# Second expert layer: where the dots' gelu stands in ScalarE's program, and how thinly token steps are laid beside the choices

## The chip, the core and the metric

The kernel runs on one core of a Trainium2 chip, as one program for the whole model. The metric is the device time of one execution in microseconds (us); the number compared is the median of several executions.

## What is computed

The program runs a small transformer over 256 tokens of width 1024. Its last stage is a "peer" layer: every token chooses 128 of 16384 experts (8 heads, 16 each), and each expert is one row of a table `u` and one row of a table `v`.

```python
def peer(h, w_q, sub_keys, u, v):
    T, D = h.shape
    q = (h @ w_q).reshape(T, PEER_HEADS, 2, PEER_QDIM // 2)
    s = jnp.einsum('thpd,hpnd->thpn', q, sub_keys)
    sv, si = lax.top_k(s, PEER_TOPK)
    cand = (sv[:, :, 0, :, None] + sv[:, :, 1, None, :]).reshape(T, PEER_HEADS, PEER_TOPK * PEER_TOPK)
    fv, fi = lax.top_k(cand, PEER_TOPK)
    ...
    idx = (i1 * PEER_NKEYS + i2).reshape(T, PEER_HEADS * PEER_TOPK)
    g = jax.nn.softmax(fv, axis=-1).reshape(T, PEER_HEADS * PEER_TOPK)
    def chunk(args):
        hc, ic, gc = args
        ue = u[ic]
        ve = v[ic]
        act = jax.nn.gelu(jnp.einsum('td,ted->te', hc, ue), approximate=False)
        return jnp.einsum('te,ted->td', gc * act, ve)
```

After it, `x = x + g2 * f` and a last RMS norm give the output.

## The kernel before

The change is in `split_experts`, the last stage (it is called by `peer_1`). It computes the layer in two ways at once.

**Dense half (tokens 128 to 255).** TensorE multiplies the tokens by the whole of `u`: 128 *up tiles* of 128 x 1024 float32 (512 KB each, `rise(e)`, line 2823), ScalarE applies gelu to each product (line 2914), and then TensorE multiplies by the whole of `v`: 128 *down tiles* of 512 KB (`fall(r)`, line 2840). Up and down tiles come through a ring of four slots, in order, by SyncE's queue (`fetch`); tile j may be fetched once tile j-4 has been used. Between the two, the activations are multiplied by gates. Gates are made four tokens at a time, in 64 steps n: VectorE writes 0/1 marks (`mark(n)`, lines 2727 to 2735), TensorE multiplies them (`gates(n)`, line 2836), VectorE multiplies the activations by the result (`weigh(n)`, line 2743). Steps 0 to 31 (the first 64 experts' keys) belong to the rise, and TensorE's program has them spread behind up tiles 74 to 125: `gates(n)` stands behind up tile 74 + 53n/32. Steps 32 to 63 stand behind down tiles 0 to 54. `mark(n)` waits for `gates(n-2)`, `weigh(n)` for `gates(n)`.

**Gathered half (tokens 0 to 127).** For each of a token's 128 choices, GpSimd's queue gathers one row per token: 128 rows of 4 KB, 512 KB in one indirect DMA (line 2594). In the first table (`u`) VectorE multiplies the gathered rows by the tokens and sums: a *dot* (line 2608). In the second table (`v`) it adds the rows, weighted, to an accumulator: an *accumulation* (line 2616 for the first, 2619 for the others). Both are called *token steps*; there are 128 of each, strictly in order. The gathers go round five buffers (`ROWS` = 5): gather n is issued when step n-5 is done, whatever table it belongs to. Between the two, ScalarE applies gelu to the 128 dots (line 2924), and VectorE multiplies by the softmax weights (line 2612).

**The choices.** Before the marks VectorE finds the top 16 of every row of scores (`sixteen`, `level`, `choices`), for 2 x 4 groups. The first four groups make the indices that the gathers need. Beside this work a counter, `spend`, lays in token steps: every instruction adds its columns + 150 to `spent`, and when that reaches 1200 a dot is issued.

What holds others up in the order of the programs: ScalarE waits ahead of gelu 64 (`AT_SCORES`) until the last `level` is done, because the activations from there on overwrite the scores. Ahead of gelu 70 (`EXP_AT`) it waits for the end of the choices. TensorE waits behind up tile 72 (`SELECTED`) for the softmax weights, VectorE ahead of the marks for the turned choices. TensorE may be at most two up tiles ahead of ScalarE's gelus. The down tiles wait for all 128 gelus and the first 32 gate steps. VectorE lays token steps between the gate steps: 1 + (n % 3 < 2) in each of n = 0 to 31, dots only; 1 + n % 2 from n = 32; the rest stand in a loop behind n = 64. Then come the sums of the dense half, `turned_back` (TensorE turns the accumulator, line 2879), the sum of squares (`sum_squares`, line 426) and the norm.

Of the kernel before, what the change touches and what calls it, by code (L numbers as in the profile page):

```python
# [21 lines left out]
ACT = mybir.ActivationFunctionType  # L22
# [3 lines left out]
P = 128  # L26
# [18 lines left out]
ROWS = 5  # L45
# [404 lines left out]
def rstd_ends(k):  # L450

    for name in ("mean_square", "inverse_mean", "rstd"):
        k.count(name).ends(1)
# [2063 lines left out]
def split_experts(k, a, layer, S, finish):  # L2517

    nc, HP, NT, B, R = k.nc, 2 * HEADS, T // P, 4, RING
    DENSE, G = T - S, HEADS // 2  # L2520
    N, Q, STEPS, HALF = NKEYS, 2 * HEADS, DENSE // 4, NKEYS // 2
    U, V = Q, Q + NKEYS
    wq, u, v = a.peer_q[layer], a.peer_u[layer], a.peer_v[layer]
    rows_of = (a.peer_rows, a.peer_v.rearrange("l a b d -> (l a b) d"))
# [15 lines left out]
    idx, act_of, coef = k.rows[0:S, 1, 0:P].bitcast(U32), k.rows[0:S, 1, P:2 * P], k.rows[0:S, 1, 2 * P:3 * P]  # L2540
    first_row = k.rows[0:S, 1, 3 * P:4 * P]
    whole_ctx = k.ctx[:].rearrange("p c t -> p (c t)")
    bufs = [b[0:S] for b in (whole_ctx[:, 0:D], whole_ctx[:, D:2 * D], k.rows[:, 0], spare[:, 1],
                             k.acts[:].rearrange("p r t -> p (r t)"))]
    marks = k.scratch[:, 0:1280].bitcast(BF16).rearrange("p (r n) -> p r n", r=2)
    second = marks[:, :, 0:512].rearrange("p r (a n t) -> p r a n t", a=2, t=2)
    in_half = marks[:, :, 512:1280].rearrange("p r (m a n t) -> p r m a n t", m=3, a=2, t=2)
# [3 lines left out]
    sums = k.ps[:, 0:4].rearrange("p b (c t) -> p (b c) t", t=T)  # L2551
    back = k.ps[:, 4:8].rearrange("p b (c t) -> p (b c) t", t=T)
    order = [(table, p) for table in range(2) for p in range(P)]
    EXP_AT, SELECTED, FIRST_GATES = 70, 72, 74
    gates_after = [[n for n in range(STEPS) if FIRST_GATES + n * (N - 1 - FIRST_GATES) // STEPS == e] for e in range(N)]
    gates_under = [[n for n in range(STEPS, 2 * STEPS) if (n - STEPS) * (HALF - 8) // STEPS == r] for r in range(N)]
    FINAL, SETTLED, LEVELS, count, picks_made = 0, 0, 0, 0, 0
# [6 lines left out]
    tokens_turned, tokens_kept, ready, used, token_gelu, token_weights, turned_back = map(k.count, (  # L2564
        "tokens_turned", "tokens_kept", "choices_ready", "row_used", "token_gelu", "token_weights", "turned_back"))
# [7 lines left out]
    with nc.Block() as block:  # L2573
        @block.sync
        def _(sp):
            for j in range(R, Q):
                k.fetch(sp, j, 0, wq[j])
            for e in range(N):
                k.fetch(sp, U + e, 0, u[e])
            for e in range(N):  # L2580
                k.fetch(sp, V + e, 0, v[:, e])
            for n in range(KD // 2):
                c = slice(2 * n, 2 * n + 2)
                sp.wait_ge(normed.sem, normed.after(2 * n + 2))
                sp.dma_start(k.out[:, c], k.x[:, c]).then_inc(stored.sem, 16)
            sp.wait_ge(stored.sem, stored.after(16 * (KD // 2)))

        @block.gpsimd
        def _(pool):
            for n, (table, p) in enumerate(order):  # L2590
                if not table and p % 32 == 0:
                    pool.wait_ge(ready.sem, ready.after(p // 32 + 1))
                pool.wait_ge(used.sem, used.after(n + 1 - ROWS))
                nc.gpsimd.indirect_dma_start(bufs[n % ROWS], None, rows_of[table],
                                             bass.IndirectOffsetOnAxis(idx[:, p:p + 1], 0)).then_inc(k.row_loaded[n % ROWS].sem, 16)

        @block.vector
        def _(dve):
            step, spent, units = 0, 0, 0

            def token_step():

                nonlocal step
                n, b = step, step % ROWS
                table, p = order[n]
                dve.wait_ge(k.row_loaded[b].sem, k.row_loaded[b].after(16 * (n // ROWS + 1)))
                if not table:
                    nc.vector.tensor_tensor_reduce(bufs[b], bufs[b], tok, 1.0, 0.0, ALU.mult, ALU.add,  # L2608
                                                   act_of[:, p:p + 1]).then_inc(used.sem, 1)
                elif p == 0:  # L2610
                    dve.wait_ge(token_gelu.sem, token_gelu.after(1))
                    nc.vector.tensor_tensor(coef, coef, weight[0:S, 0:HEADS].rearrange("p n b -> p (n b)"),
                                            ALU.mult).then_inc(token_weights.sem, 1)
                    dve.wait_ge(token_weights.sem, token_weights.after(1))
                    dve.wait_ge(used.sem, used.after(n))
                    nc.vector.tensor_scalar(tok, bufs[b], coef[:, p:p + 1], None, ALU.mult).then_inc(used.sem, 1)
                else:
                    dve.wait_ge(used.sem, used.after(n))
                    nc.vector.scalar_tensor_tensor(tok, bufs[b], coef[:, p:p + 1], tok, ALU.mult, ALU.add).then_inc(used.sem, 1)  # L2619
                step += 1  # L2620

            def spend(columns):

                nonlocal spent
                if units:
                    spent += columns + 150
                    if spent >= 1200 and step < min(P, 32 * units):
                        spent -= 1200
                        token_step()

            def sixteen(rows, src, rest, values, places, arrive):
# [106 lines left out]
            def weigh(n):  # L2738

                h, n_of_half = n // STEPS, n % STEPS  # L2740
                acts = A[:, h * HALF:(h + 1) * HALF, n_of_half * B:(n_of_half + 1) * B]
                dve.wait_ge(product.sem, product.after(n + 1))
                nc.vector.tensor_tensor(acts, acts, k.ps[:, gate_bank(n), 0:B * HALF].rearrange("p (t n) -> p n t", t=B),
                                        ALU.mult).then_inc(kept.sem, 1)
# [29 lines left out]
            for n in range(2 * STEPS + 1):  # L2774
                if n < 2 * STEPS:
                    mark(n)
                if n:
                    weigh(n - 1)
                for _ in range(1 + (n % 3 < 2) if n < STEPS else 1 + n % 2):
                    if step < (P if n < STEPS else len(order)):  # L2780
                        token_step()
            while step < len(order):
                token_step()
            for c in range(KD):
# [101 lines left out]
        @block.scalar  # L2886
        def _(act):
            def take(j):

                act.wait_ge(done.sem, done.after(j + 1))  # L2890
                nc.scalar.activation(q[:, j], k.ps[:, j % R, 0:T], ACT.Copy).then_inc(taken.sem, 1)

            def move(p):

                act.wait_ge(scored.sem, scored.after(p + 1))
                nc.scalar.activation(s.rearrange("p (t r) n -> p t r n", t=NT)[:, :, 2 * p:2 * p + 2].rearrange(
                    "p t r n -> p t (r n)"), k.ps[:, 6 + p % 2].rearrange("p (t n) -> p t n", t=NT), ACT.Copy).then_inc(moved.sem, 1)

            take(0)
            act.wait_ge(tokens_turned.sem, tokens_turned.after(1))  # L2900
            for n in range(2):
                nc.scalar.activation(tok[:, n * 4 * P:(n + 1) * 4 * P], k.ps[0:S, 4 + n], ACT.Copy).then_inc(tokens_kept.sem, 1)
            for j in range(1, Q):
                take(j)
                if j >= 3 and j % 2:
                    move(j // 2 - 1)
            for e in range(N):
                if e == AT_SCORES:
                    act.wait_ge(top.sem, top.after(LEVELS))
                if e == EXP_AT:  # L2910
                    act.wait_ge(after.sem, after.after(SETTLED))
                    nc.scalar.activation(weight, weight, ACT.Exp).then_inc(exps.sem, 1)
                act.wait_ge(done.sem, done.after(U + e + 1))
                nc.scalar.activation(A[:, e], k.ps[:, 4 + e % 2, 0:DENSE], ACT.Gelu).then_inc(acted.sem, 1)  # L2914
                if e == 0:
                    move(HEADS - 1)
                if e == SELECTED:
                    for w in range(3):
                        act.wait_ge(transposed.sem, transposed.after(3 * NT))
                        nc.scalar.activation(k.picks[:, :, w],  # L2920
                                             k.ps[:, 6 + w // 2, w % 2 * T:w % 2 * T + T].rearrange("p (s t) -> p s t", t=B),
                                             ACT.Copy).then_inc(picked.sem, 1)
            act.wait_ge(used.sem, used.after(P))
            nc.scalar.activation(coef, act_of, ACT.Gelu).then_inc(token_gelu.sem, 1)
            for c in range(KD):
                act.wait_ge(settled.sem, settled.after(c + 1))
                square_x(k, c, 1)
            root_of_inverse(k, act)
# [19 lines left out]
    for c in (turned_back, settled, normed, k.count("squares")):  # L2948
        c.ends(KD)
    rstd_ends(k)  # L2950
    for b in range(ROWS):
        k.row_loaded[b].ends(16 * len(range(b, len(order), ROWS)))
    tables.ends(16)
    stored.ends(16 * (KD // 2))
    k.ring_ends(V + N, 0)
# [254 lines left out]
```

## Time and profile before

| | us |
|---|---|
| median of 3 runs | 3766.13 (3762.77 to 3767.57) |
| the profiled execution | 3757.47 |
| its span, first to last instruction | 3755.7 |
| `split_experts`, from about 2984 to the end of the span | 772 |
| TensorE busy over the span | 3287.2 (88%) |
| VectorE busy | 2497.0 (66%) |
| ScalarE busy | 874.4 (23%) |
| DMA | 983.68 MB, mean 262 GB/s |

The times in rows are microseconds from the start of the span. The span is a single profiled execution, 8.66 us faster than the median of the timed ones, and 1.8 us of it lie outside the span. The busy share of an engine over the whole span says little of the last stage, so the stage is read in windows.

### The profile page before, as it was taken

To read this page: it belongs to the slowest core of one execution; us is meant where nothing else is said; L and a number is where in the kernel's file an instruction comes from. 1 tells how busy PE (TensorE), PEld (TensorE's weight loads), DVE (VectorE), ACT (ScalarE), POOL (GpSimd) and SP (SyncE) were. 2 spreads that over 40 slices of the span, in tenths; PEclk is the share of its full clock that TensorE was granted. 3 is DMA by queue.
4 is the path that set the end of the run, shared out by engine and by line. 5 is a ranking of instruction groups with operands and counts; after the bars stand their busy time and mean duration, and the time that the engine had idled before them with its cause. 6 is when DMAs were issued, how large, how long until landed. Compare 5 with 4: busy or idle time off the path is not lost. (4 is left out here: it accounts for less than half of the span.)

```text
span 3755.7 us, 56484 instructions
## 1 busy us (share of the span) xinstructions
PE 3287.2 (88%) x22342; PEld 2862.1 (76%) x22359; DVE 2497.0 (66%) x4759; ACT 874.4 (23%) x1601; POOL 883.1 (24%) x804
## 2 busy tenths in 40 slices
PE   9998999998999978999499987778879897599876
PEld 9976999986997657887388866666657687488875
DVE  5556656555664364589988857767775488877745
ACT  4345434334443353111022200000014411110000
POOL 0000000000000001014555545555530033423432
PEclk9999999999999999999799999999999999899998
DMA  7652666642662204279899999999971289999998
GB/s 245 224 176 101 234 222 205 230 160 90 230 211 84 73 1 152 73 234 394 306 355 369 363 364 403 400 403 404 404 290 49 97 336 409 349 361 342 406 409 316
DMA packets 298406, 983.68 MB, mean 262 GB/s; under 512 B 32928, under 2 KB 66720, under 8 KB 297248
## 3 DMA queue, kind: packets, MB, share of 16 engines
q1 hardware_dynamic: 187552, 577.36, 43.6%
q0 software_dynamic: 110592, 402.70, 27.6%
q8 instruction: 179, 2.93, 0.3%
q14 instruction: 83, 0.68, 0.1%
HBM read 960.01 MB, written 19.92 MB: 261 GB/s over the span
## 5 line engine op out<-in xcount | busy, mean ns | idle before, releaser
L325 PE MATMUL banks<-h_whole,ring 128*128 128x256 f32 (+1 forms) x4352 | 782.6, 336 | 138.0 <-ACT acts_out L2459 54.0
L325 PEld LDWEIGHTS banks<-h_whole,ring 128*128 128x128 f32 x4352 | 677.1, 193 | 214.4 <-ACT big L2914 84.7
L300 DVE TENSOR_TENSOR ring_lo<-ring,ring_hi 128x1024 fp32r<-128x1024 f32 x365 | 448.0, 1228 | 370.4 <-ACT ring_hi L294 351.1
L325 PE MATMUL banks<-scratch,ring 128*128 128x256 f32 x2048 | 490.1, 396 | 126.6 <-DVE scratch L2269 126.3
L325 PEld LDWEIGHTS banks<-scratch,ring 128*128 128x128 f32 x2048 | 392.8, 196 | 224.0 <-DVE scratch L2269 171.2
L294 ACT ACTIVATE ring_hi<-ring 128x1024 fp32r<-128x1024 f32 x365 | 386.7, 1059 | 571.1 <-PE banks L315 512.2
L325 PE MATMUL banks<-big,ring 128*128 128x128 f32 x2048 | 260.8, 281 | 50.7 <-DMA ring<-peer_v_dram 47.8
L311 PE MATMUL banks<-h_parts,ring_hi 128*128 128x256 f32 x1160 | 287.2, 286 | 6.0 <-PEq L664 3.4
L325 PEld LDWEIGHTS banks<-big,ring 128*128 128x128 f32 x2048 | 238.0, 192 | 70.2 <-DMA ring<-peer_v_dram 66.8
L312 PE MATMUL banks<-h_parts,ring_hi 128*128 128x256 f32 x1160 | 283.8, 282 | 0.0
L311 PEld LDWEIGHTS banks<-h_parts,ring_hi 128*128 128x128 f32 x1160 | 221.7, 191 | 18.3 <-issue 17.8
L984 POOL TENSOR_TENSOR scratch<-ctx_t 128x256 f32<-128x256 f32 x8 | 7.9, 991 | 929.7 <-POOLq L609 929.7
L312 PEld LDWEIGHTS banks<-h_parts,ring_hi 128*128 128x128 f32 x1160 | 221.7, 191 | 0.3
L2104 POOL DMA_INDIRECT x_t<-peer_rows_dram,rows x103 | 129.5, 1258 | 346.0 <-DVE rows L2218 211.6
L311 PE MATMUL banks<-h_parts_ctx,ring_hi 128*128 128x256 f32 x768 | 189.9, 285 | 4.3 <-ACT ring_hi L294 4.3
L312 PE MATMUL banks<-h_parts_ctx,ring_hi 128*128 128x256 f32 x768 | 187.7, 282 | 0.0
L2134 DVE SCALAR_TENSOR_TENSOR h_whole<-x_t,rows,h_whole 128x1024 f32<-128x1024 f32 x102 | 130.8, 1284 | 57.4 <-DMA x_t<-peer_v_dram,rows 57.0
L2134 DVE SCALAR_TENSOR_TENSOR h_whole<-ctx_t,rows,h_whole 128x1024 f32<-128x1024 f32 x101 | 129.8, 1285 | 57.2 <-DMA ctx_t<-peer_v_dram,rows 56.7
L315 PE MATMUL banks<-h_parts,ring_lo 128*128 128x256 f32 x1160 | 163.0, 283 | 0.1
L312 PE MATMUL banks<-hidden_parts,ring_hi 128*128 128x256 f32 x672 | 162.9, 281 | 0.0
L311 PE MATMUL banks<-hidden_parts,ring_hi 128*128 128x256 f32 x672 | 162.8, 281 | 0.0
L311 PEld LDWEIGHTS banks<-h_parts_ctx,ring_hi 128*128 128x128 f32 x768 | 146.6, 191 | 13.8 <-issue 13.5
(366 smaller groups left out, 5852.5 us busy)
## 6 DMA issues: line engine op xcount, KB each, us to landing
ring<-peer_u_dram SPq DMA_DIRECT2D x256, 512.0 KB
ring<-peer_v_dram SPq DMA_DIRECT2D x256, 512.0 KB
big<-mod_w_dram SPq DMA_DIRECT2D x96, 512.0 KB, 4.6
ring<-ffn_gate_dram SPq DMA_DIRECT2D x88, 512.0 KB
ring<-ffn_up_dram SPq DMA_DIRECT2D x88, 512.0 KB
ring<-ffn_down_dram SPq DMA_DIRECT2D x88, 512.0 KB
ring<-peer_q_dram SPq DMA_DIRECT2D x32, 512.0 KB
act_store<-acts_out SPq DMA_DIRECT2D x128, 128.0 KB
```

The lines of the kernel that those rows point to most:

```text
L294: self.nc.scalar.activation(self.hi[:, n % 2], self.ring[:, self.slot(j)], ACT.Copy).then_inc(self.count("tile_hi").sem, 1)
L300: self.nc.vector.tensor_tensor(self.lo[:, self.slot(j)], self.ring[:, self.slot(j)], self.hi[:, n % 2].bitcast(F32), ALU.subtract).then_in ...
L311: self.nc.tensor.matmul(out, w, b_hi, start=opens and m == 0, stop=False)
L312: self.nc.tensor.matmul(out, w, b_lo, start=False, stop=False)
L315: ins = self.nc.tensor.matmul(out, self.lo[:, self.slot(j), c * P:(c + 1) * P], b_hi, start=False, stop=opens and m == last)
L325: ins = self.nc.tensor.matmul(out, self.ring[:, self.slot(j), c * P:(c + 1) * P], b, start=opens and m == 0, stop=opens and m == len(terms ...
L984: k.nc.gpsimd.tensor_tensor(to, norm.src[:, c], norm.src[:, c], ALU.mult).then_inc(squared.sem, 1)
L2104: nc.gpsimd.indirect_dma_start(bufs[n % ROWS], None, rows_of[n // TOKEN_STEPS], bass.IndirectOffsetOnAxis(idx[:, t, p:p + 1], 0)).then_inc ...
L2134: nc.vector.scalar_tensor_tensor(tok[:, t], bufs[b], coef[:, t, p:p + 1], tok[:, t], ALU.mult, ALU.add).then_inc(used.sem, 1)
```

## The change

Four edits, all in `split_experts`. The number of gather buffers is taken from the list `bufs` (which has five) and not from `ROWS` (which is 5). `spend` issues a dot each 1500 and not each 1200. In the marks' loop, each n has 1 + (n % 3 < 2) token steps throughout; at n = 20 all dots that are left are done; accumulations may begin at n = 24. ScalarE's gelu of the dots stands behind gelu 112 of the up tiles and not behind the last.

```diff
@@ -2542,6 +2542,7 @@
+    W = len(bufs)
@@ -2551,7 +2552,7 @@
-    EXP_AT, SELECTED, FIRST_GATES = 70, 72, 74
+    EXP_AT, SELECTED, FIRST_GATES, GELU_AT, DOTS_BY = 70, 72, 74, 112, 20
@@ -2590,9 +2591,9 @@
             for n, (table, p) in enumerate(order):
                 if not table and p % 32 == 0:
                     pool.wait_ge(ready.sem, ready.after(p // 32 + 1))
-                pool.wait_ge(used.sem, used.after(n + 1 - ROWS))
-                nc.gpsimd.indirect_dma_start(bufs[n % ROWS], None, rows_of[table],
-                                             bass.IndirectOffsetOnAxis(idx[:, p:p + 1], 0)).then_inc(k.row_loaded[n % ROWS].sem, 16)
+                pool.wait_ge(used.sem, used.after(n + 1 - W))
+                nc.gpsimd.indirect_dma_start(bufs[n % W], None, rows_of[table],
+                                             bass.IndirectOffsetOnAxis(idx[:, p:p + 1], 0)).then_inc(k.row_loaded[n % W].sem, 16)
@@ -2624,8 +2625,8 @@
                 if units:
                     spent += columns + 150
-                    if spent >= 1200 and step < min(P, 32 * units):
-                        spent -= 1200
+                    if spent >= 1500 and step < min(P, 32 * units):
+                        spent -= 1500
                         token_step()
@@ -2776,9 +2777,11 @@
                     mark(n)
                 if n:
                     weigh(n - 1)
-                for _ in range(1 + (n % 3 < 2) if n < STEPS else 1 + n % 2):
-                    if step < (P if n < STEPS else len(order)):
+                for _ in range(1 + (n % 3 < 2)):
+                    if step < (P if n < DOTS_BY + 4 else len(order)):
                         token_step()
+                while n == DOTS_BY and step < P:
+                    token_step()
             while step < len(order):
                 token_step()
@@ -2914,14 +2917,15 @@
                 if e == 0:
                     move(HEADS - 1)
+                if e == GELU_AT:
+                    act.wait_ge(used.sem, used.after(P))
+                    nc.scalar.activation(coef, act_of, ACT.Gelu).then_inc(token_gelu.sem, 1)
                 if e == SELECTED:
                     ...
-            act.wait_ge(used.sem, used.after(P))
-            nc.scalar.activation(coef, act_of, ACT.Gelu).then_inc(token_gelu.sem, 1)
```

The other hunks put `W` for `ROWS` in the buffer's number and in the semaphores' last counts.

## Rows read from the trace of the kernel before

**Rows 1.** The page's slices of the span: DMA's busy share in 40 slices.

```profile
DMA  7652666642662204279899999999971289999998
```

**Rows 2.** Windows: stretch, length, busy (count) of each engine, PEclk, DMA share, GB/s.

```profile
3080.00:3200.00 120.00, 93.30 (x738) 85.90 (x739) 102.60 (x293) 12.86 (x47) 45.67 (x47) 1.00 1.03 409
...
3218.00:3250.00 32.00, 3.57 (x24) 3.35 (x24) 30.20 (x91) 0.45 (x2) 13.57 (x14) 0.59 0.86 293
3250.00:3281.00 31.00, 22.43 (x145) 21.59 (x144) 27.61 (x67) 6.03 (x14) 15.43 (x15) 0.82 0.95 356
...
3351.00:3406.00 55.00, 53.36 (x597) 52.96 (x597) 23.86 (x71) 7.61 (x28) 0.00 (x0) 1.00 0.82 254
3406.00:3420.00 14.00, 13.21 (x147) 12.89 (x148) 12.74 (x25) 0.08 (x1) 6.76 (x5) 1.00 0.90 316
3420.00:3440.00 20.00, 16.49 (x166) 15.39 (x167) 15.24 (x30) 0.00 (x0) 9.21 (x8) 1.00 1.01 402
3440.00:3460.00 20.00, 17.93 (x183) 16.94 (x182) 16.04 (x31) 0.00 (x0) 8.99 (x7) 1.00 1.00 371
...
3720.00:3736.00 16.00, 6.38 (x51) 5.60 (x49) 11.50 (x10) 0.00 (x0) 5.83 (x5) 0.89 0.83 301
```

**Rows 3.** The same stretch for two lines alone: the gathers (2594), gelu (2914).

```profile
3080.00:3200.00 120.00, 45.67 (x47) 1.00 1.03 409
...
3080.00:3200.00 120.00, 12.86 (x47) 1.00 1.03 409
```

**Rows 4.** Timeline, ScalarE: start, us, what [idle before <-releaser]: gelu 63; 64 and 65.

```profile
3215.54 0.28 ACT L2914 ACTIVATE big<-banks 128x128 f32<-128x128 f32 x1 [2.28 <-PE banks L325]
3248.18 0.45 ACT L2914 ACTIVATE big<-banks 128x128 f32<-128x128 f32 x2 [32.36 <-DVE big L2650]
```

**Rows 5.** Timeline, VectorE beside the choices: dots 1, 17, 75, 79 and 89.

```profile
3031.75 1.23 DVE L2608 CUSTOM_DVE_ANT_0 ctx_t<-ctx_t,h_whole 128x1024 f32<-128x1024 f32 x1 [2.73 <-DMA ctx_t<-peer_rows_dram,rows]
...
3066.06 1.23 DVE L2608 CUSTOM_DVE_ANT_0 ctx_t<-ctx_t,h_whole 128x1024 f32<-128x1024 f32 x1
...
3217.32 1.22 DVE L2608 CUSTOM_DVE_ANT_0 acts_out<-acts_out,h_whole 128x1024 f32<-128x1024 f32 x1
...
3227.40 1.23 DVE L2608 CUSTOM_DVE_ANT_0 h_whole<-h_whole 128x1024 f32<-128x1024 f32 x1 [0.55 <-DMA h_whole<-peer_rows_dram,rows]
...
3248.80 1.22 DVE L2608 CUSTOM_DVE_ANT_0 h_whole<-h_whole 128x1024 f32<-128x1024 f32 x1
```

**Rows 6.** Timeline, VectorE: the last dot, and the weights behind the dots' gelu.

```profile
3339.53 1.22 DVE L2608 CUSTOM_DVE_ANT_0 rows<-rows,h_whole 128x1024 f32<-128x1024 f32 x1
...
3406.18 0.29 DVE L2612 TENSOR_TENSOR rows<-rows,big 128x128 f32<-128x128 f32 x1 [3.81 <-ACT rows L2924]
```

**Rows 7.** Timeline, GpSimd: the sixth gather of the second table.

```profile
3407.53 0.94 POOL L2594 DMA_INDIRECT h_whole<-peer_v_dram,rows  x1 [65.57 <-DVE h_whole L2616]
```

**Rows 8.** Timeline, TensorE: up tiles (16 matmuls each) behind two waits, gates, tiles with data waiting.

```profile
3248.51 10.32 PE L325 MATMUL banks<-h_whole,ring 128*128 128x128 f32 x64 [27.89 <-ACT big L2914]
...
3268.10 3.63 PE L325 MATMUL banks<-h_whole,ring 128*128 128x128 f32 x16 [3.67 <-ACT big L2914]
...
3356.72 3.82 PE L325 MATMUL banks<-h_whole,ring 128*128 128x128 f32 x32
3360.38 0.52 PE L2836 MATMUL banks<-scratch 128*128 128x64 bf16 x12
```

**Rows 9.** Timeline, VectorE: two accumulations in a row, in the marks' loop.

```profile
3425.66 2.67 DVE L2619 SCALAR_TENSOR_TENSOR h_whole<-ctx_t,rows,h_whole 128x1024 f32<-128x1024 f32 x2
```

**Rows 10.** Timeline, TensorE: the last down tile, the turned accumulator, two sums of squares.

```profile
3725.76 2.05 PE L325 MATMUL banks<-big,ring 128*128 128x128 f32 x16 [0.48 <-DMA ring<-peer_v_dram]
...
3736.70 1.97 PE L2879 MATMUL banks<-con,h_whole 128*128 128x128 f32 x8 [8.83 <-DVE h_whole L2619]
3740.84 6.33 PE L426 MATMUL banks<-big,ones 128*128 128x256 f32 x16 [2.17 <-DVE x_t L2789]
...
2973.66 3.72 PE L1794 MATMUL banks<-big,ones 128*128 128x256 f32 x16 [0.49 <-ACT big L1775]
```

More of the change, by code:

```diff
@@ L2603, in token_step @@
                 nonlocal step
-                n, b = step, step % ROWS
+                n, b = step, step % W
                 table, p = order[n]
-                dve.wait_ge(k.row_loaded[b].sem, k.row_loaded[b].after(16 * (n // ROWS + 1)))
+                dve.wait_ge(k.row_loaded[b].sem, k.row_loaded[b].after(16 * (n // W + 1)))
                 if not table:
@@ L2950, in split_experts @@
     rstd_ends(k)
-    for b in range(ROWS):
-        k.row_loaded[b].ends(16 * len(range(b, len(order), ROWS)))
+    for b in range(W):
+        k.row_loaded[b].ends(16 * len(range(b, len(order), W)))
     tables.ends(16)
```

## The prediction

> **What bounds the kernel now.** I read the slices of the page first, then the last stage in windows, then the timelines of single engines where the windows show a hole. The slices show DMA near its full share from slice 33 on, with two dips [rows 1]. In windows the full rate is 409 GB/s, at a DMA share of 1.03, as from 3080 to 3200 [rows 2]. One tile or one gather is 128 x 1024 float32 = 524,288 bytes, so at full rate each costs 524,288 / 409,000 = 1.28 us. I call that a *unit*. The stage moves 128 up tiles, 128 down tiles and 256 gathers, 512 units. That is 656 us of the 772 the stage lasts, so the DMA engines bound it, and a time is won only where they are idle. In 120 us 47 gathers and 47 gelus of up tiles pass [rows 3]: with both queues backed up the two streams share the engines one to one, a tile and a gather in each 2.56 us.
>
> Where DMA is below 409 GB/s, the shortfall over 409 times the length is lost time [rows 2]:
> - 3218 to 3250, 293 GB/s: 32 x 116/409 = 9.1 us; 3250 to 3281, 356 GB/s: 4.0 us. Together **13.1 us**.
> - 3351 to 3406, 254 GB/s: 20.8 us; 3406 to 3420, 316 GB/s: 3.2 us. Together **24.0 us**.
> - 3420 to 3460, 402 and 371 GB/s: **2.2 us**. 3720 to 3736, 301 GB/s: **4.2 us**.
>
> The sum is 43.5 us. The first hole is ScalarE's wait ahead of gelu 64: gelu 63 starts at 3215.54, gelu 64 at 3248.18, released by VectorE's last `level` after 32.36 us idle [rows 4]. TensorE is 27.89 us without work [rows 8], the ring is full, and only gathers are left. The second hole is the dots' gelu: the last dot starts at 3339.53, the weights behind the gelu at 3406.18 [rows 6], the next gather waits 65.57 us [rows 7]. Up tiles alone use 254 of 409 GB/s, since TensorE bounds them: two tiles start at 3356.72 and the gates behind them at 3360.38 [rows 8], so it needs 1.8 us a tile, and about 0.4 for a gate step of 0.52 that overlaps the next tile, against 1.28 of DMA a tile.
>
> **Part 1: dots at 1500.** Counting `spend` through the program: when the last `level` is done, 88 dots stand before it with 1200 and 70 with 1500. At the end of the choices it is 97 and 77, ahead of the marks 103 and 83. Does thinning bring the choices forward? Before, dots 17 to 75 take 3217.32 - 3066.06 = 151.3 us, 2.61 us each, and dots 79 to 89, with no wait for data in between, 21.4 us, 2.14 us each [rows 5]. A dot holds VectorE for 1.15 us (1.22 less the overlap), so 1200 of `spend` are 0.99 us and 1500 are 1.24. Then a dot with its share of the choices takes 2.39 us, still below the 2.6 that the shared DMA allows. So the gathers keep their pace, VectorE uses the idle time that it has beside them, and dot 70 falls where it did: dots 1 to 17 take 0.25 us more each from 3031.75 [rows 5], so dot 16 stands at about 3066.5, and 54 dots at 2.6 us later dot 70 stands at 3207. **The last level is ready at about 3209**, ahead of gelu 64, which up tiles at 2.56 us bring at 3218.1. The wait of 32 us is gone. What is next late? Dot 77, the end of the choices, at about 3226, against gelu 69 at 3231. The exp then waits for nothing, three dots and the shares end near 3236, and TensorE finishes up tile 72 at 3238.5. The marks begin near 3243, up tile 74 needs them at 3244. Each has 2 to 9 us in hand, and a stall below the 3 tiles in the ring (7 us) costs DMA nothing. I take 1 us lost, for a thinner start. W is 5 as before: nothing.
>
> **Part 2: dots by n = 20.** Before, 14 gate steps finish the dots; now 20 leave 117 done, and 11 are drained in n = 20. Up tile 105, behind which gates(19) stands, ends at 3215.5 + 42 x 2.56 = 3323, so the drain starts at 3324. VectorE could do it in 11 x 1.15 = 12.7 us, but the rows come by DMA. TensorE goes on with tiles 106 to 108 and stops at about 3331 for mark 21, which is queued on VectorE behind the drain; the ring fills with 109 to 112. So some 10.5 gathers and 6.5 tiles have to land, 17 units, 21.8 us: **the drain ends at about 3346**, and mark 21 (1.4 us) at 3347.5. TensorE idles 16 us, DMA doesn't. Then four tiles and three gate steps up to gates(23) would take 8.4 us at 1.8 and 0.4. After 27.89 us idle four tiles took 10.32 us, and after 3.67 us idle one took 3.63, where PEclk is 0.59 and 0.82 [rows 2, 8]: the clock was at its lower level (1.2 GHz). I take 12 us: the first accumulation at 3360. In these 14 us from the drain's end, 11 units, DMA has the five gathers of the second table that may be ahead, less one, and some 3 to 4 tiles: **about 4 us lost**. The gelu at 112 itself waits for nothing: tile 112 follows the drain in TensorE's program. It is 0.3 us of ScalarE.
>
> The Trainium skill speaks against such a pause (TensorE: Matmul & The Clock Gate, "The HAM clock gate"): the clock is gated to half while the array is idle and is given back after busy time. By the page the four tiles cost what I took for them and no more; without any gating the 4 us would be 1. The trace agrees in the two rows named.
>
> **Part 3: accumulations from n = 24.** Steps 24 to 31 bring 14 of them beside tiles 113 to 127. A gate step of VectorE's is 23.86 us / 14 steps = 1.7 us in 3351 to 3406, of five instructions each (71 in all) [rows 2], an accumulation 1.33 (2.67 for two) [rows 9]; 1.7 + 5/3 x 1.33 = 3.9 us a step, against 5/3 gathers and 53/32 tiles, 3.3 units, 4.26 us. DMA is full again. The down tiles start near 3394 (before: 3406.9), with 14 accumulations done where there were none. I take 2 us lost at this passage. From n = 32 the gate step has 1.67 accumulations instead of 1.5 and 1.75 tiles: 4.38 us of DMA to 3.9 of VectorE. The small holes of 2.2 us I leave.
>
> **Part 4: the end.** At n = 64 there were 177 token steps done, now 197: 59 left, beside 72 tiles. Before, the down tiles ended first (3727.8) and TensorE waited 8.83 us for the last accumulation [rows 10]. Now gathers end about 12 tiles before TensorE, which then takes 1.8 us a tile instead of 1.28: 12 x 0.52 = **6 us lost**, plus 0.5 us because a last tile takes 1.8 us after landing and a last accumulation 1.3. In exchange TensorE comes to the sum of squares without the 8.8 us pause. It took 6.33 us there and takes 3.72 for the same 16 matmuls elsewhere [rows 10]: 2.6 us won, if the clock is the cause.
>
> **Sum.** Lost before 43.5; lost after 1 + 4 + 2 + 2.2 + 6 + 0.5 = 15.7, and 1 more for what VectorE's lumpy work does to the pace: 16.7. Gain 43.5 - 16.7 + 2.6 = **29.4 us**: 3757.5 - 29.4 = 3728.1 for an execution like the profiled one, whose span would be 3726.3. Against the median of the runs, 8.7 us higher, 3766.1 - 29.4 = **3736.7**.
>
> **Rivals.**
> - *The second hole only moves.* The drain holds TensorE, and then TensorE holds the stage: gathers of the second table come too late to fill anything, as when the drain ends at 3360 and not 3346 because gathers keep to one in 2.56 us (11 x 2.56 = 28 us) with the ring long full. Then DMA idles for 10 us in the drain and 7 behind it, and the gain is 29.4 - 15: 3751. Against it: with the ring full nothing competes with the gathers, and VectorE's dots are at 1.15 us. For it: 3218 to 3250 ran at 293 GB/s with gathers alone [rows 2], though there VectorE had 1 us of choices between dots. Chance 0.14.
> - *The choices are still late* (the change doesn't do what it says at gelu 64). It takes 2.8 us a dot to pass 3218. Each 0.1 us above that costs 5 us of wait, of which DMA loses 0.3. At 3.0 us, 10 us of wait: 4 us lost, within the forecast's own range; that it comes to the old wait would need 3.2. Then the gain is about 16: 3750. Chance 0.05.
> - *Slower: TensorE stays at the lower clock behind the drain.* A tile at that level takes 3.63 us against 2.56 of shared DMA, so each tile beyond the first four costs 1.07. The gain is used up after 29.4/1.07 = 27 tiles, and if it lasts through the marks of the second half (15 + 56 tiles) it costs 76: 3813. Up to 20 tiles it is 3737 to 3758. Against it: after the two waits of before PEclk is 0.59 and 0.82 and then 1.00 again [rows 2]. Chance 0.04 beyond 27 tiles, 0.04 for 10 to 27.
> - *More is won*: the drain starts with several rows landed, no slow tiles behind it, and the streams end together. Lost after is then 7 and the gain 39: 3727, down to 3721. Chance 0.10.
>
> **How the numbers follow.** Forecast (gain 20 to 37 us, 3729 to 3746) 0.60; the cases above 0.37; unnamed 0.03. The range 3721 to 3757 takes in the forecast, the larger gain and the two rivals that keep half of it. A measurement of this kernel tells 0.2%, 7.5 us, from no change. Below 3758.6 lie the forecast, the larger gain and most of the first two rivals: faster 0.86; same 0.07; slower 0.07.
>
> **What would show it.** Gelu 64 in ScalarE's timeline at about 3218 with no idle over 3 us; the last dot at 3345; TensorE idle 14 to 18 us ahead of tile 109; the weights (line 2612) at about 3360; the first down tile near 3394; the last accumulation about 20 us before the last down tile; DMA at 409 GB/s in all windows but those just named. Wrong if the window 3324 to 3346 is below 380 GB/s (first rival), if gelu 64 starts after 3225 (second), or if PEclk is below 1 past 3375 (third).

## The result, and the profile after

The changed kernel takes 3737.4 us in the median of 6 runs (3734.2 to 3742.2), the kernel before 3760.7 (3754.1 to 3767.6, also 6): a ratio of 0.9938, 95% interval 0.9923 to 0.9952, so 23.3 us or 0.6% less. The profiled execution took 3737.35 us with a span of 3735.5.

The spans differ by 20.2 us, but the last stage doesn't start at the same time in each execution. Its first instruction that is easy to find is ScalarE's first copy of the queries. In ScalarE's timeline (columns: start, duration, engine and line, operation, in brackets the idle time ahead and what ended it) it stands, before and after, at

```profile
2991.87 0.39 ACT L2891 ACTIVATE big<-banks 128x256 f32<-128x256 f32 x1 [7.94 <-PE banks L325]
```

```profile
2995.20 0.39 ACT L2894 ACTIVATE big<-banks 128x256 f32<-128x256 f32 x1 [7.94 <-PE banks L325]
```

From there to the end of the span I count the *stage*: 3755.7 - 2991.87 = 763.8 us before and 3735.5 - 2995.20 = 740.3 after. The stage is 23.5 us shorter, about as the medians are, and the 3.3 us lie ahead of it, in work that the change doesn't touch. The experiments below are compared by the stage too, since it leaves that scatter out; but each stage comes from one profiled execution, and its own scatter is known from a single repeat (740.3 and 739.7 us for the changed kernel). Of what stands later in after than in the forecast, 3.3 us are this later start.

Windows of after (columns: the window, its length, busy us and instructions of PE, PEld, DVE, ACT, POOL, then the granted clock, the DMA share and GB/s):

```profile
3036.00:3216.00 180.00, 145.81 (x1105) 134.66 (x1104) 172.72 (x544) 22.81 (x72) 73.18 (x73) 0.99 1.02 406
3216.00:3236.00 20.00, 15.17 (x122) 13.85 (x120) 14.14 (x32) 2.05 (x8) 7.46 (x8) 1.00 1.03 409
3236.00:3256.00 20.00, 17.16 (x163) 16.36 (x164) 15.00 (x36) 6.04 (x14) 8.14 (x8) 1.00 0.97 371
3256.00:3334.00 78.00, 67.30 (x703) 63.23 (x700) 65.10 (x152) 8.33 (x30) 28.87 (x31) 1.00 1.02 407
3334.00:3380.00 46.00, 26.45 (x273) 25.91 (x269) 32.56 (x65) 3.53 (x13) 19.32 (x17) 0.78 0.90 318
3380.00:3420.00 40.00, 35.46 (x356) 33.25 (x356) 32.53 (x61) 2.50 (x9) 15.79 (x15) 1.00 1.02 403
3420.00:3540.00 120.00, 105.52 (x1076) 98.54 (x1076) 100.62 (x181) 0.00 (x0) 61.66 (x46) 1.00 1.02 406
3540.00:3697.00 157.00, 125.53 (x990) 114.18 (x991) 79.09 (x63) 0.00 (x0) 56.65 (x58) 1.00 1.02 406
3697.00:3720.00 23.00, 23.00 (x207) 22.94 (x206) 0.98 (x4) 0.00 (x0) 0.00 (x0) 1.00 0.72 238
```

Lost time again is the shortfall from 409 GB/s over 409, times the length. The two holes of before, 13.1 and 24.0 us [rows 2], are gone. In their place stand 20 x 38/409 = 1.9 us at 3236 to 3256, and 46 x 91/409 = 10.2 us around the drain. The windows at 403 to 407 GB/s lose 4.3 us together. At the end 14 down tiles run alone, and 3697 to 3720 loses 23 x 171/409 = 9.6 us.

ScalarE's timeline is the answer to [rows 4]. Gelu 64 (the second line) has no wait left but for its tile, and the exp ahead of gelu 70 follows gelu 69 at once:

```profile
3219.61 0.28 ACT L2917 ACTIVATE big<-banks 128x128 f32<-128x128 f32 x1 [2.29 <-PE banks L325]
3222.23 0.28 ACT L2917 ACTIVATE big<-banks 128x128 f32<-128x128 f32 x1 [2.34 <-PE banks L325]
...
3235.89 0.28 ACT L2917 ACTIVATE big<-banks 128x128 f32<-128x128 f32 x1 [2.26 <-PE banks L325]
3236.19 1.28 ACT L2915 ACT_TABLE_LOAD   x1
3237.49 0.42 ACT L2915 ACTIVATE big<-big 128x256 f32<-128x256 f32 x1
```

TensorE's timeline answers [rows 8] and [rows 10]:

```profile
3334.58 2.02 PE L325 MATMUL banks<-h_whole,ring 128*128 128x128 f32 x16 [0.22 <-DMA ring<-peer_u_dram]
3354.42 0.82 PE L2839 MATMUL banks<-scratch 128*128 128x64 bf16 x12 [17.82 <-DVE scratch L2736]
3355.05 6.38 PE L325 MATMUL banks<-h_whole,ring 128*128 128x128 f32 x32
3361.27 0.52 PE L2839 MATMUL banks<-scratch 128*128 128x64 bf16 x12
3361.63 3.82 PE L325 MATMUL banks<-h_whole,ring 128*128 128x128 f32 x32
...
3404.34 1.83 PE L325 MATMUL banks<-big,ring 128*128 128x128 f32 x15
...
3694.91 25.41 PE L325 MATMUL banks<-big,ring 128*128 128x128 f32 x224 [0.44 <-DMA ring<-peer_v_dram]
3720.21 1.04 PE L2882 MATMUL banks<-con,h_whole 128*128 128x128 f32 x8
3723.30 3.72 PE L426 MATMUL banks<-big,ones 128*128 128x256 f32 x16 [2.04 <-DVE x_t L2792]
```

TensorE stands 17.82 us for mark 21 (line 2736), which is queued behind the drain. Two tiles at the lower clock take 6.38 us, the next two 3.82. At the end 224 matmuls, 14 tiles, run without a gap, 1.81 us each.

VectorE's timeline shows the drain's first, fourth and last dot, the weights, the first accumulation (line 2617) and the second, the last one, and the wait of the dense half's sums:

```profile
3333.76 1.22 DVE L2609 CUSTOM_DVE_ANT_0 rows<-rows,h_whole 128x1024 f32<-128x1024 f32 x1
...
3341.16 1.22 DVE L2609 CUSTOM_DVE_ANT_0 ctx_t<-ctx_t,h_whole 128x1024 f32<-128x1024 f32 x1 [1.34 <-DMA ctx_t<-peer_rows_dram,rows]
...
3351.81 1.23 DVE L2609 CUSTOM_DVE_ANT_0 rows<-rows,h_whole 128x1024 f32<-128x1024 f32 x1 [0.15 <-DMA rows<-peer_rows_dram,rows]
...
3366.19 0.28 DVE L2613 TENSOR_TENSOR rows<-rows,big 128x128 f32<-128x128 f32 x1
3366.51 0.75 DVE L2617 TENSOR_SCALAR h_whole<-h_whole,rows 128x1024 f32<-128x1024 f32 x1
3367.36 1.28 DVE L2620 SCALAR_TENSOR_TENSOR h_whole<-acts_out,rows,h_whole 128x1024 f32<-128x1024 f32 x1
...
3695.38 1.28 DVE L2620 SCALAR_TENSOR_TENSOR h_whole<-ctx_t,rows,h_whole 128x1024 f32<-128x1024 f32 x1 [1.21 <-DMA ctx_t<-peer_v_dram,rows]
3719.02 2.16 DVE L2789 SCALAR_TENSOR_TENSOR x_t<-banks,mods,x_t 128x128 f32<-128x128 f32 x8 [22.36 <-PE banks L325]
```

### The profile page after: what moved, and what is told of

It is laid out like the page before. It is cut to its first block and busy times, and to the rows that moved or that the text cites. A ratio compares the mean times of both kernels' runs of the same rounds, so it can differ in the third digit from the quotient of the medians.

```text
span 3735.5 us, 56501 instructions
## 1 busy us (share of the span) xinstructions
PE 3296.8 (88%) x22359; PEld 2870.9 (77%) x22359; DVE 2492.0 (67%) x4759; ACT 874.7 (23%) x1601; POOL 885.7 (24%) x804
## 5 line engine op out<-in xcount | busy, mean ns | idle before, releaser
L325 PE MATMUL banks<-scratch,ring 128*128 128x256 f32 x2048 | 502.4, 404 | 120.7 <-DVE scratch L2269 120.3
L325 PEld LDWEIGHTS banks<-scratch,ring 128*128 128x128 f32 x2048 | 405.3, 202 | 217.9 <-DVE scratch L2269 159.6
L311 PEld LDWEIGHTS banks<-h_parts_ctx,ring_hi 128*128 128x128 f32 x768 | 146.5, 191 | 13.8 <-issue 13.5
```

Of the source, the lines that this page charges most:

```text
L311: self.nc.tensor.matmul(out, w, b_hi, start=opens and m == 0, stop=False)
L325: ins = self.nc.tensor.matmul(out, self.ring[:, self.slot(j), c * P:(c + 1) * P], b, start=opens and m == 0, stop=opens and m == len(terms ...
```

## Experiments

The theory: the stage is as long as its 512 units plus the time in which DMA idles, at its start, in the holes and at its end. That sum holds for any stage that moves the same bytes; what has to be found out is which edit opens or closes which hole. The gain is the two holes removed, less what the drain and the end give back. The experiments ask which part of the change won the time, what made DMA idle behind the drain, and whether drain and end can be had cheaper. All were timed beside the kernel before; ratios are against it.

**Thinning alone.** The kernel before with one number changed:

```diff
-                    if spent >= 1200 and step < min(P, 32 * units):
-                        spent -= 1200
+                    if spent >= 1500 and step < min(P, 32 * units):
+                        spent -= 1500
```

> The kernel before with 1500 for 1200 in spend and nothing else: the dots' gelu stays behind the last up tile, accumulations begin with the down tiles. Theory (a time is won only where DMA idles): the wait ahead of gelu 64 goes (13 us of idle DMA), and the 20 dots that are moved fill part of the second hole by themselves: dots last to gate step 26 instead of 14, and only some 9 up tiles run alone, about 6 us idle instead of 24. The gain is then 20 to 28 us, as much as the whole change: ratio to the kernel before 0.9930 to 0.9950. Rival (the gelu's new place earns the second half of the gain): only the first hole goes, 12 to 14 us, ratio 0.9965.

Measured: 3732.0 us, ratio 0.9933 (0.9920 to 0.9947); stage 736.4. One number brings as much as the whole change, in the profile 3.9 us more. The first hole is gone. The second shrinks from 24.0 us to 10.5 (I had expected 6), though the dots' gelu still stands behind tile 127: 20 dots more are left for the gate steps, and their gathers fill the stretch in which there was nothing to gather. So with and without part 2 some 10 us are lost there. The thinned kernel is better off at its end: DMA loses 4.6 us there (292 GB/s in 3694.3 to 3710.3) and not 9.6, though the sum of squares, at 6.51 us and behind a wait of 9.02, takes a part of that back. Its windows:

```profile
3216.00:3256.00 40.00, 31.67 (x282) 29.53 (x282) 30.97 (x70) 8.03 (x21) 15.82 (x16) 1.00 1.02 404
3360.00:3380.00 20.00, 18.74 (x194) 18.00 (x192) 8.05 (x25) 2.28 (x9) 0.00 (x0) 1.00 0.87 297
3380.00:3400.00 20.00, 17.02 (x176) 16.18 (x177) 16.08 (x32) 0.41 (x2) 9.14 (x7) 1.00 0.92 336
3400.00:3420.00 20.00, 18.19 (x195) 17.31 (x194) 15.51 (x29) 0.00 (x0) 8.05 (x6) 1.00 1.00 380
```

**The gelu's place and the early accumulations alone.** The changed kernel with 1200 in `spend`, as it was. The loop at n = 20 then has nothing to do, since the dots end at n = 14, so this run says nothing of the drain:

```diff
-                    if spent >= 1500 and step < min(P, 32 * units):
-                        spent -= 1500
+                    if spent >= 1200 and step < min(P, 32 * units):
+                        spent -= 1200
```

> The changed kernel with 1200 in spend: only the gelu behind tile 112 and the new marks' loop are left. No dots are left to drain at n = 20 (all are done at n = 14). Theory: the wait ahead of gelu 64 stays (32 us, 13 us of DMA), the second hole is shortened from gate steps 14 to 32 to steps 14 to 24, so 24 us idle become 12 to 14, and 3 us are given back where the gathers end before the down tiles. Gain 5 to 9 us, ratio 0.9976 to 0.9987. Rival (the gelu's place earns most): the second hole goes whole, gain 20 us or more, ratio below 0.9950.

Measured: 3752.2 us (11 runs), ratio 0.9985 (0.9976 to 0.9995); stage 756.7, 7.1 less than before. The first hole stays (the lines below: 3.5 and 7.7 us, and 2.4 more in 3280 to 3300); around the second, 331 GB/s in 3330 to 3380 and 360 in 3380 to 3400 are 11.9 us lost. So the two parts don't add: 27.4 us of stage for thinning alone, 7.1 for the rest alone, 23.5 together. Each halves the second hole by itself, and together they leave 10.2 us of it, since only with both is there a drain, which the next run takes away.

```profile
3220.00:3240.00 20.00, 3.09 (x26) 2.74 (x24) 18.17 (x46) 0.00 (x0) 8.34 (x9) 0.66 0.93 338
3240.00:3260.00 20.00, 8.12 (x49) 8.12 (x50) 19.97 (x68) 1.00 (x4) 8.43 (x9) 0.57 0.79 251
```

**Without the drain.** Two dots in each gate step up to n = 23 and no loop at n = 20:

```diff
-                for _ in range(1 + (n % 3 < 2)):
+                for _ in range(2 if n < DOTS_BY + 4 else 1 + (n % 3 < 2)):
                     if step < (P if n < DOTS_BY + 4 else len(order)):
                         token_step()
-                while n == DOTS_BY and step < P:
-                    token_step()
```

> The changed kernel without the drain: two dots in each gate step up to n = 23 (all 128 are done at n = 22) instead of 5/3 with 11 left over at n = 20. Theory: the drain stops TensorE for 17.8 us, and behind it DMA ran at 318 and 291 GB/s for 40 us (10 us lost). With the same dots spread, TensorE has no stop over 4 us, and 6 to 9 us of these 10 come back: ratio to the kernel before 0.9912 to 0.9925 where the whole change has 0.9938. Rival (the idle is only put elsewhere, since the dots end as early and up tiles run alone behind them): within 2 us of the changed kernel, ratio 0.9933 to 0.9943.

Measured: 3728.6 us, ratio 0.9927 (0.9913 to 0.9940); stage 729.5, 10.8 less than with the drain. In the profile the gain is more than I expected; the timed ratio is just above my range. The profiled execution is the fastest of its five. By the ratios, 0.9927 against 0.9938 and 0.9945 for two series of the changed kernel, the gain is 4 to 7 us, and the intervals overlap. DMA holds 400 GB/s where it had 318, and 14 tiles still stand alone at the end:

```profile
3340.00:3380.00 40.00, 35.02 (x358) 33.96 (x359) 34.71 (x72) 4.35 (x16) 18.62 (x15) 0.96 1.02 400
```

```profile
3682.49 25.28 PE L325 MATMUL banks<-big,ring 128*128 128x128 f32 x224 [0.46 <-DMA ring<-peer_v_dram]
```

**Is it the clock?** The changed kernel, with 60 products of zeros that keep TensorE busy while it waits for mark 21:

```diff
+                    if n == DOTS_BY + 1:
+                        k.idle_products(6, 60)
```

> The changed kernel, with 60 matmuls on zeros into an unused bank ahead of gate step 21, so that TensorE is busy while it waits for the drain (some 13 us of 17.8). Theory: behind the drain PEclk was at its lower level and two tiles took 6.38 us instead of 3.6; DMA was at 291 GB/s there because TensorE gave the ring's slots back late. With the clock kept up the two tiles take 3.8 and 2 to 3 us of the stage come back: 737 to 738 us where the changed kernel has 740.3. Rival (the idle DMA behind the drain is set by the full ring and the end of the gathers, not by the clock): two tiles at 3.8 us, but the stage within 1 us of 740.3.

Measured: 3735.5 us, ratio 0.9936 (0.9923 to 0.9950); stage 739.8 against 740.3, where the theory had 737 to 738. The rival is right on the stage. The clock was kept up only in part: the two tiles behind the wait take 4.89 us instead of 6.38, not 3.8, and the granted clock in 3354 to 3362 is 0.82 instead of 0.60. The first accumulation starts 1.9 us earlier (3364.59, the last line of the first view below, against 3366.51; the restart itself was 0.4 earlier). But in 3334 to 3378 DMA idles 9.9 us, where it idled 10.2 without.

```profile
3334.80 13.11 PE L276 MATMUL banks<-con,zeros 128*128 128x512 bf16 x60
3354.00 0.82 PE L2839 MATMUL banks<-scratch 128*128 128x64 bf16 x12 [6.09 <-DVE scratch L2736]
3354.63 4.89 PE L325 MATMUL banks<-h_whole,ring 128*128 128x128 f32 x32
...
3364.59 0.75 DVE L2617 TENSOR_SCALAR h_whole<-h_whole,rows 128x1024 f32<-128x1024 f32 x1
```

```profile
3346.00:3354.00 8.00, 1.91 (x10) 0.69 (x8) 6.44 (x15) 0.00 (x0) 5.88 (x6) 0.75 0.88 293
3354.00:3362.00 8.00, 8.00 (x76) 7.99 (x77) 4.78 (x15) 0.77 (x3) 0.00 (x0) 0.82 0.78 266
3362.00:3370.00 8.00, 8.00 (x99) 7.96 (x98) 5.76 (x11) 1.28 (x6) 3.10 (x3) 1.00 0.81 269
```

**An even end.** The changed kernel with fewer accumulations beside the second half's marks, so that gathers and down tiles end together:

```diff
-                for _ in range(1 + (n % 3 < 2)):
+                for _ in range(1 + (n % 3 < 2) if n < STEPS else 1 + (n % 4 == 0)):
```

> The changed kernel with 1.25 accumulations in each gate step from n = 32 (40 in the second half and not 53), so that 13 more gathers are left for the time behind the marks. Theory: in the changed kernel the last 14 down tiles ran alone at 1.81 us where DMA needs 1.28, 7.4 us lost; now gathers and down tiles end within about 4 tiles of each other and 3 to 6 us come back, ratio to the kernel before 0.9920 to 0.9932. Rival (a gate step of 1.75 tiles and 1.25 gathers leaves DMA idle, since TensorE needs 3.6 us for it and DMA 3.8): nothing is won, ratio 0.9935 to 0.9945.

Measured: 3743.7 us, ratio 0.9964 (0.9950 to 0.9977); stage 740.6. The end is even: the last accumulation starts at 3719.66, the last two tiles at 3718.69. But that wins nothing, since DMA now idles beside the marks: seven windows from 3420 to 3560 run at 355 to 400 GB/s, of which three stand here, and lose 8.3 us. TensorE, which has gate steps on top of its tiles there, is busy for 17.7 to 19.0 of each 20 us in the first six; that it is what holds DMA back there is likely, but not tested.

```profile
3420.00:3440.00 20.00, 18.15 (x197) 17.49 (x196) 14.40 (x27) 0.00 (x0) 5.90 (x5) 1.00 0.96 355
...
3480.00:3500.00 20.00, 18.72 (x206) 18.28 (x204) 16.19 (x34) 0.00 (x0) 7.41 (x7) 1.00 0.98 375
3500.00:3520.00 20.00, 17.68 (x189) 16.89 (x190) 13.50 (x28) 0.00 (x0) 6.41 (x6) 1.00 1.01 386
```

The timed median is some 6 us worse than the changed kernel's while the stage of the profiled run is equal. The profiled execution is the fastest of its five, and the intervals of the two ratios touch; more isn't known.

**No drain, and one and a half accumulations beside the marks.** The version without the drain, with the old rhythm from n = 32: 1.5 accumulations a gate step, between the 5/3 of the change and the 5/4 of the even end:

```diff
-                for _ in range(2 if n < DOTS_BY + 4 else 1 + (n % 3 < 2)):
+                for _ in range(2 if n < DOTS_BY + 4 else 1 + (n % 3 < 2) if n < STEPS else 1 + n % 2):
```

> The kernel without the drain, and from n = 32 with 1 + n % 2 accumulations, 48 in the second half instead of 53. Without the drain the stage took 729.5 us and some 17 down tiles ran alone at its end (8 to 9 us lost). Theory: five more gathers at the end shorten that by 5 tiles, 2.5 us, and the marks' second half keeps DMA full, as it was in the kernel before (2.2 us lost in 40): stage 727 to 728. Rival, from the even end: what is won at the end is lost beside the marks, 729 to 730.

Measured: 3728.1 us, ratio 0.9913 (0.9898 to 0.9929); stage 727.9, as expected, though one profile each doesn't tell it from the 729.5 without the drain. The changed kernel, run again beside it on the same chip, had 3736.1 us, ratio 0.9945 (0.9931 to 0.9959), stage 739.7. The two intervals don't overlap, and each of its five times is below each of the other's, so this version is shown to beat it: by 8 us in the medians, 12 in the ratios and 11.8 in the stages. DMA is full at 3340 to 3380 (407 GB/s) and beside the marks (406), and 8 tiles stand alone at the end instead of 14:

```profile
3698.21 14.56 PE L325 MATMUL banks<-big,ring 128*128 128x128 f32 x128 [0.30 <-DMA ring<-peer_v_dram]
```

**Thinner still.** The kernel before with 1800, nothing else:

```diff
-                    if spent >= 1200 and step < min(P, 32 * units):
-                        spent -= 1200
+                    if spent >= 1800 and step < min(P, 32 * units):
+                        spent -= 1800
```

> The kernel before with 1800 for 1200 in spend and nothing else. 70 dots stand ahead of the marks (83 with 1500, 103 before), so the dots at 5/3 a gate step last to step 34 and the second hole is filled by dots alone, with the gelu where it was. Theory: with 1500 the stage took 736.5 us, of it 10 us in windows of 297, 336 and 380 GB/s around the last gelu; these go, VectorE's dot with its choices is 2.64 us, a little over the 2.56 of shared DMA, which up tiles take up: stage 727 to 730 us, ratio 0.9905 to 0.9925, as good as the kernel without the drain. Rival (accumulations begun ahead of the down tiles are what is worth having, and more dots late make the gates late): 735 us or more.

Measured: 3733.6 us (6 runs), ratio 0.9931 (0.9917 to 0.9944); stage 734.5, between my 727 to 730 and the rival's 735: a miss. The second hole closes without any change to the gelu or the gate steps, but the choices are now ready too early. VectorE stands 24.15 us for the exp that ScalarE has ahead of gelu 70, and no dot is laid in a wait, so the gathers stop:

```profile
3235.15 0.42 DVE L2716 TENSOR_REDUCE big<-big 128x16 f32<-128x256 f32 x1 [24.15 <-ACT big L2912]
```

```profile
3220.00:3240.00 20.00, 19.36 (x172) 19.01 (x171) 4.44 (x9) 6.24 (x15) 2.19 (x2) 1.00 0.85 302
3380.00:3400.00 20.00, 17.78 (x178) 16.38 (x177) 15.13 (x36) 0.59 (x2) 8.47 (x7) 1.00 1.02 405
```

**In between, and an earlier exp.** The kernel before with 1650 in the same two lines; and the version with 1800 with the exp ahead of gelu 60:

> The kernel before with 1650 in spend and nothing else, between 1500 (stage 736.5 us) and 1800 (734.5). 76 dots stand ahead of the marks, so the dots last to gate step 30 of 32, and the choices end later than with 1800. Theory: the second hole shrinks from about 10 us (1500) to 3, and VectorE's wait for the exp from the 24.15 us of 1800, which cost 5 us of DMA, to about 12, which five gathers ahead nearly cover. Stage 729 to 732 us. Rival (the time depends little on spend once the first wait is gone): 734 to 737.

```diff
-    EXP_AT, SELECTED, FIRST_GATES = 70, 72, 74
+    EXP_AT, SELECTED, FIRST_GATES = 60, 63, 67
```

> The kernel with 1800 in spend, and the exp ahead of gelu 60 (not 70), the turned choices behind up tile 63 (not 72), the first gate step behind tile 67 (not 74). With 1800 VectorE waited 24.15 us for the exp and DMA was at 302 GB/s for 20 us. Theory: VectorE waits under 8 us for the exp, the window comes back to 380 GB/s or more and 3 to 5 us of the stage are won: 730 to 732 us where it was 734.5. Rival (the thinner start, 387 and 383 GB/s in the first 40 us, and not the exp, is why 1800 was no better): 733.5 us or more.

Measured for 1650: 3729.6 us, ratio 0.9919 (0.9906 to 0.9932), stage 737.7, just above the rival's 734 to 737: VectorE still waits 15.9 us for the exp (346 and 380 GB/s in 3216 to 3256), and part of the second hole stays (367 in 3370 to 3410). Measured with the early exp: 3733.0 us, ratio 0.9927 (0.9914 to 0.9939), stage 733.3. The wait's window is back at 395 GB/s, where 302 had cost 5.2 us, but the stage is only 1.2 us shorter than without: not the 730 to 732 I had expected, and next to the rival's 733.5. The time came back as small losses elsewhere, such as 394 and 398 GB/s in 3040 to 3080 and 378 in 3380 to 3400.

**All together.** The version with 8 tiles at the end, with 1650, two dots in each gate step until all are done (n = 25), and the gelu at tile 120:

```diff
-    EXP_AT, SELECTED, FIRST_GATES, GELU_AT, DOTS_BY = 70, 72, 74, 112, 20
+    EXP_AT, SELECTED, FIRST_GATES, GELU_AT, DOTS_BY = 70, 72, 74, 120, 24
```

> 1650 in spend, two dots in each gate step until all are done (n = 25), the dots' gelu behind gelu 120, accumulations from n = 28, 1 + n % 2 of them from n = 32. Against the kernel without the drain and with 48 accumulations in the second half (stage 727.9 us, 3728.1 us), fewer accumulations are ahead when the down tiles begin, so fewer down tiles are left alone at the end (12 there). Theory: no stretch over 10 us below 380 GB/s ahead of the last tiles, under 8 tiles alone, stage 724 to 727 us, ratio to the kernel before 0.9900 to 0.9915. Rival: what the end gains the 1650 loses beside the choices, 727 to 730 us.

Measured: 3727.9 us (6 runs), ratio 0.9918 (0.9904 to 0.9932), stage 729.9: the rival's figure, no better than with 1500 (727.9). VectorE waits 16.0 us for the exp here too (347 and 356 GB/s in 3220 to 3260). Each ratio has an interval of about 0.14% to either side, so the versions between 0.9913 and 0.9933 aren't told apart by their times.

## Why the prediction was right, and where its sum was off

The forecast was 3736.7 us, faster by 29.4. The time came out at 3737.4, but partly by luck: the median of before, 3766.1 in the runs that I started from, is 3760.7 with the later ones, and the gain was 23.3. The sign and the mechanism were right, and the gain was 6 us too large.

- **Bound by DMA: right, but the count left something out.** Lost time was 43.5 us before by the prediction's count. That passes over windows of 404 to 408 GB/s, 2.2 us together. With them it is 45.7 us up to 3736 before, and 26.1 up to 3720 after: 1.9 beside the choices, 10.2 around the drain, 9.6 at the end, 4.4 in the windows at 399 to 408. That is 19.6 us less. From the turned accumulator to the end of the span it is 19.0 us before and 15.3 after, 3.7 less, of which 2.6 lie in the sum of squares. Together that is 23.3 of the 23.5 us of the stage.
- **Part 1, the choices: right.** Gelu 64 stands at 3222.2, forecast 3218.1 and 3.3 us of late start: 0.8 us off. Thinning alone brings as much as the whole change, so this part carries it. I took nothing lost at the passage to the marks; 1.9 us were lost beside the end of the choices, where VectorE waited 2.69 us for the exp that I had waiting for nothing.
- **Part 2, start and length of the drain: nearly.** 11 dots, 19.2 us plus the mark, where I had 22. It starts at 3333.8, which is 6.5 us late on the stage's clock: tile 105 came 2 us late, and VectorE, which I took to be 1 us behind gates(19) (TensorE, 3328.7), still had dots of n = 19 to do. TensorE's pause was 17.8 us, within the 14 to 18 that I named.
- **Part 2, the end of the drain and what follows it: mis-sized.** I had 14 us from its end to the first accumulation, and it was 13.5 (3352.96 to 3366.51). But for the lost DMA I took 4 us, and 2 for the passage behind it; it was 10.2. 2.7 us of them went before the drain was over (350 GB/s in 3334 to 3353), where I had nothing. I had the drain at full rate to its end, although [rows 2] had gathers alone with a full ring at 293 GB/s; here they ran at 270. Then 4.7 us went up to the first accumulation (268 GB/s in 3353 to 3366.5), and 2.9 us up to 3378 (307 GB/s). The finer windows are below. Behind the drain the streams came one after the other. Of the five gathers that may be ahead, GpSimd's queue moved 1.79 MB, 3.4 gathers, only in 3354 to 3362; SyncE's queue moved nothing in 3346 to 3358 and was alone in 3362 to 3366, at 202 GB/s. I had also laid part of the 4 us to the lower clock ("without any gating the 4 us would be 1"). The run with the zeros speaks against that: 1.5 of the 2.6 us that two tiles lose at the lower clock came back (6.38, 4.89, 3.82), and behind 3354 DMA idled 6.6 us instead of 7.4. What the rest would bring, no run shows.

```profile
3346.00:3354.00 8.00, 0.00 (x0) 0.00 (x0) 7.74 (x15) 0.00 (x0) 5.85 (x6) 0.50 0.78 270
3354.00:3362.00 8.00, 7.58 (x59) 7.57 (x60) 3.66 (x13) 0.56 (x2) 1.02 (x1) 0.60 0.82 284
3362.00:3370.00 8.00, 8.00 (x90) 7.98 (x90) 5.45 (x14) 1.09 (x5) 2.17 (x2) 1.00 0.80 226
3370.00:3378.00 8.00, 7.03 (x81) 6.92 (x80) 7.76 (x15) 1.05 (x4) 4.81 (x4) 1.00 0.96 341
```

- **Part 3: right after the passage.** 403 to 406 GB/s from 3380 on. The first down tile starts at 3404.3, forecast 3394 and 3.3: 7 us late, as the drain was.
- **Part 4, the end: right in kind, mis-sized.** 14 tiles alone instead of 12. At 0.53 us each that is 7.4 us instead of 6.5. But the windows, by which the 4.2 us of before were counted, give 9.6: the last tile is in the ring early, and DMA has 97 GB/s in 3715 to 3720 while TensorE works off what lies there. The sum of squares took 3.72 us, and the 2.6 us are won. The condition of the forecast ("if the clock is the cause") fits: the granted clock was 0.58 beside it before and 1.00 after.
- **The rivals.** The first (the hole only moves) asked for 10 us lost in the drain and 7 behind it. The drain lost 2.7, so the first half didn't happen; the second did, with 7.5 behind it. Neither late choices nor a lasting lower clock (1.00 again from 3362) were seen. The clock rule of the Trainium skill (TensorE: Matmul & The Clock Gate, "The HAM clock gate") holds for the tiles: the granted clock was 0.50 and 0.60 around the restart. That it costs the kernel anything is not shown: with the zeros two tiles were 1.5 us faster and the stage 0.5, which is what a repeat differs by.

What the prediction didn't ask at all is whether part 2 is needed once part 1 is made. The early accumulations fill a hole that the 20 moved dots already half fill, and the drain brings a pause of its own. With the drain spread out part 2 looks worth having in the stages: 736.4 us for thinning alone, 740.3 with the drain, 729.5 without, 727.9 with the old rhythm beside the second marks. The times agree in order (0.9933, 0.9938, 0.9927, 0.9913), but their intervals tell only the last from the changed kernel as run beside it (0.9945), and not from thinning alone.

Still open: why the profiled stage and the timed median rank some variants differently (the even end, and 1650 against 1800). The stage's start alone lies between 2991.9 and 3001.2 us in the thirteen profiled executions, which is more than these versions differ by, and a median of five or six may carry a part of it.

## What to carry to other kernels

Where DMA is the bound, keep a ledger of its idle time, and ask of two edits whether they fill the same hole: the work moved by one edit can make the other needless. Draining one stream's work in one piece stops every engine that waits for work queued behind it, and the two streams then refill one after the other; with the same work spread over the steps before, the profiled stage was 10.8 us shorter here, and the timed gain 4 to 7 us. Balance between streams counts only while both are moving: here an even finish won nothing, since the stretch before it ran below the full rate.

## What the runs showed of the hardware

Two streams side by side (tiles by SyncE's queue, gathers by GpSimd's) reach 409 GB/s. Gathers alone with the ring full didn't, though VectorE took a row block in 1.25 us and GpSimd issued 6 in 8 us: 270 GB/s in 3346 to 3354, and 293 in the same window of the run with the zeros. What holds them there is not shown. Keeping TensorE busy with 60 products of zeros in a 17.8 us pause raised the granted clock of the 8 us behind it only from 0.60 to 0.82 (the products had ended 6.09 us before the gate step), and the 1.5 us by which two tiles were faster came with a stage 0.5 us shorter, no more than a repeat differs by.
